# Key norms of the second block: sums with ones on the stationary side, roots and inverses on all partitions

## What is computed

```python
def rms_norm_2(x, g):
    xf = x.astype(jnp.float32)
    y = xf * lax.rsqrt(jnp.mean(xf * xf, axis=-1, keepdims=True) + EPS)
    return (y * g.astype(jnp.float32)).astype(x.dtype)

def split_kv(p_kv, k_norm_a, k_norm_b):
    b, n = p_kv.shape[:2]
    k_a, v_a, k_b, v_b = jnp.split(p_kv, [A_KV, 2 * A_KV, 2 * A_KV + B_QK], axis=-1)
    k_a = rms_norm_2(k_a.reshape(b, n, A_KV_HEADS, A_HEAD_DIM), k_norm_a)
...
    k_b = rms_norm_2(k_b.reshape(b, n, B_HEADS, 2, B_HEAD_DIM), k_norm_b)
```

## Time and profile before

| | |
|---|---|
| median of 3 runs | 2992.62 us (2988.23 to 2994.47) |
| the profiled execution | 2988.73 us |
| its span, first to last instruction | 2986.8 us |
| mean granted clock of the PE | 0.991 |
| stage `q` within it | 1463.4 to 1634.9 us |

### The profile page before, as it was taken

The page is one execution under the profiler, slowest core; times in us unless marked ns, Lnnn a source line. Parts: engine busy times, 40 slices in busy tenths (PEclk is TensorE's granted clock), DMA queues, the critical chain, the costliest instruction groups (busy, mean ns, idle before and its releaser), DMA issues.

```text
span 2986.8 us, 54566 instructions
## 1 busy us (share of the span) xinstructions
PE 2867.2 (96%) x19302; PEld 2614.9 (88%) x19302; DVE 1888.8 (63%) x2292; ACT 1595.0 (53%) x2360; POOL 787.2 (26%) x646
## 2 busy tenths in 40 slices
PE   8998899899999999999999999989989999999999
PEld 8998899898899988888888888889988888888888
DVE  5666677766677776533355666766776765555554
ACT  5555566545577765332344666665656654344443
POOL 2554234203344421121102421244424530000000
PEclk9999999999999999999999999999999999999999
DMA  7874677667777776344556655577767876666665
GB/s 264 265 241 134 204 240 240 191 183 232 242 249 244 241 240 202 95 144 146 155 167 185 191 168 161 176 241 232 243 217 243 263 257 186 188 185 188 183 187 164
DMA packets 174445, 610.65 MB, mean 204 GB/s; under 512 B 19200, under 2 KB 27520, under 8 KB 173952
## 3 DMA queue, kind: packets, MB, share of 16 engines
q1 hardware_dynamic: 161856, 589.37, 62.9%
q10 hardware_dynamic: 11152, 14.61, 1.6%
q0 software_dynamic: 1328, 5.24, 0.5%
HBM read 598.66 MB, written 5.77 MB: 202 GB/s over the span
## 4 chain that ended last, share of the span: by engine, by line
PE 70%; DVE 10%; ACT 8%; DMA 6%; issue 5%; DVEq 0%; ACTq 0%; SPq 0%
PE acc L1624 20%; PE acc L1628 19%; PE acc L1626 9%; PE acc L1627 9%; DVE wlo L1048 4%; ACT whi L603 3%; DMA raw<-w_ada 3%; ACT cond_products L599 2%; DVE conv_out L1142 1%; PE acc L1612 1%; PE acc L1614 1%; PE acc L1615 1%; PE sums L1846 1%; PE acc L1622 1%; PE sums L1682 1%
## 5 line engine op out<-in xcount | busy, mean ns | idle before, releaser
L1048 DVE TENSOR_TENSOR wlo<-raw,whi 128x1024 fp32r<-128x1024 f32 x864 | 1134.7, 1323 | 862.9 <-ACT whi L603 861.5
L603 ACT ACTIVATE whi<-raw 128x1024 fp32r<-128x1024 f32 x864 | 908.3, 1057 | 930.1 <-PE acc L1628 515.9
L1628 PE MATMUL acc<-operand,wlo 128*128 128x256 f32 (+1 forms) x4816 | 1399.0, 290 | 0.0
L1626 PE MATMUL acc<-operand,whi 128*128 128x256 f32 (+1 forms) x3136 | 938.2, 299 | 74.7 <-DVE wlo L1048 49.1
L1628 PEld LDWEIGHTS acc<-operand,wlo 128*128 128x128 f32 x4816 | 924.9, 192 | 14.3
L1627 PE MATMUL acc<-operand,whi 128*128 128x256 f32 (+1 forms) x3136 | 927.1, 296 | 0.0
L1626 PEld LDWEIGHTS acc<-operand,whi 128*128 128x128 f32 x3136 | 606.3, 193 | 99.5 <-DVE wlo L1048 48.3
L1627 PEld LDWEIGHTS acc<-operand,whi 128*128 128x128 f32 x3136 | 606.8, 194 | 12.5
L1624 PE MATMUL acc<-operand,whi 128*128 128x512 f32 x1680 | 601.6, 401 | 9.6 <-DVE operand L1392 5.9
L466 POOL TENSOR_TENSOR cond_products<-cond_products 128x512 f32<-128x512 f32 x192 | 255.6, 1331 | 1293.7 <-ACT cond_products L599 1293.1
L1624 PE MATMUL acc<-ffn_act,whi 128*128 128x512 f32 x1344 | 473.6, 396 | 3.8 <-DVE wlo L1048 3.6
(11 more groups left out here) (219 smaller groups left out, 2469.6 us busy)
## 6 DMA issues: line engine op xcount, KB each, us to landing
raw<-w_ada SPq DMA_DIRECT2D x256, 512.0 KB, 4.4
raw<-w_in SPq DMA_DIRECT2D x224, 512.0 KB, 4.0
raw<-w_up SPq DMA_DIRECT2D x176, 512.0 KB, 4.5
raw<-w_down SPq DMA_DIRECT2D x88, 512.0 KB, 4.4
raw<-w_fg SPq DMA_DIRECT2D x88, 512.0 KB, 4.2
raw<-w_fu SPq DMA_DIRECT2D x88, 512.0 KB, 3.7
raw<-w_fd SPq DMA_DIRECT2D x88, 512.0 KB, 3.5
raw<-w_o SPq DMA_DIRECT2D x32, 512.0 KB, 4.3
```

What stands on the lines that cost most here:

```text
L603: act.activation(whi[j % RING][:], raw[j % RING][:], ACT.Copy).then_inc(hi_done, 2 if st.entries[j % st.upb - 1] == (None, ADA_VEC) else 1)
L1048: dve.tensor_tensor(wlo[j % RING][:], raw[j % RING][:], whi[j % RING][:].bitcast(F32), ALU.subtract).then_inc(lo_done, 2 if prev[0] is Non ...
L1626: pe.matmul(out_, h[:, x, f], mov[:, 0], start=first, stop=False)
L1628: ins = pe.matmul(out_, l[:, x, f], mov[:, 0], start=False, stop=last)
```

## The change

The query chunks go on as before, with counters of their own order (`Q_ORDER`). For the key chunks:

- PE, steps t+3 and t+4: `key_sums`. The whole block of ones (or `halves`) is the stationary operand, two tiles of squares, 512 columns, the moving one. The result has the sum of a column on all its partitions. A chunk takes two such matmuls ("half" 0 and 1), and both write the bank `AB`, so each waits for the root of the one before (`k_root`).
- ACT, steps t+3 and t+4: the root of each half, 128x512, from `AB` to two tiles of `R` (40 to 43 for even chunks, 44 to 47 for odd ones), at the end of the step's work.
- DVE, steps t+4 (one), t+5 (two) and t+6 (one): reciprocals of the four tiles, 128x256 each, in place. At t+7 `scale_keys` reads them in place of `TP`.
- `broadcast` and its semaphore are gone. ACT's low half of the last four groups (`b >= 4`) also waits for the scaled chunks, since tiles 40 to 47 are queries' from there on. Before stage `gates` the PE waits for the values' copies and the last key root.

```diff
@@ -375,6 +376,8 @@
+        Q_ORDER = [c for c in CH_ORDER if c >= NK]
+        inverses = lambda c: 40 + 4 * (c % 2)
...
@@ -638,6 +641,8 @@
                     act.wait_ge(v2_turned, 2 * b + gb + 1)
+                    if b >= 4:
+                        act.wait_ge(n_scaled, b + 1)
...
@@ -855,19 +860,33 @@
-                    if i >= 2:
-                        act.wait_ge(n_sum, i - 1)
+                    if i >= 2 and CH_ORDER[i - 2] < NK:
+                        act.wait_ge(k_sum, 2 * CH_ORDER[i - 2] + 2)
+                    elif i >= 2:
+                        act.wait_ge(n_sum, Q_ORDER.index(CH_ORDER[i - 2]) + 1)
...
+                    if c >= NK:
+                        act.wait_ge(n_sum, Q_ORDER.index(c) + 1)
+                        act.activation(HR[:, hr_cols(c)], NB[:, hr_cols(c)], ACT.Sqrt, bias=SM[:, EPS_C:EPS_C + 1],
+                                       scale=1.0 / (64 if CH[c][1] else HD)).then_inc(n_root, 1)
+                for half in range(2):
+                    for i, c in job_at(s, 3 + half):
+                        if c < NK:
+                            act.wait_ge(k_sum, 2 * c + half + 1)
+                            act.wait_ge(v2_turned, 12 if c % 2 else 10)
+                            if c >= 2:
+                                act.wait_ge(n_scaled, c - 1)
+                            t = inverses(c) + 2 * half
+                            act.activation(R[:, t:t + 2, :], AB[:].rearrange("p (a n) -> p a n", a=2), ACT.Sqrt,
+                                           bias=SM[:, EPS_C:EPS_C + 1],
+                                           scale=1.0 / (64 if CH[c][1] else HD)).then_inc(k_root, 1)
...
@@ -1433,11 +1452,16 @@
-                dve.wait_ge(n_bcast, c + 1)
+                dve.wait_ge(k_inv, 4 * c + 4)
                 dve.scalar_tensor_tensor(
                     out=chunk, in0=chunk, scalar=gain_col("k_b" if br else "k_a", 0),
-                    in1=TP[:].rearrange("p k (a n) -> p k a n", a=2), op0=ALU.mult,
-                    op1=ALU.mult).then_inc(n_scaled, 1)
+                    in1=quad(R[:, inverses(c):inverses(c) + 4, :]), op0=ALU.mult, op1=ALU.mult).then_inc(n_scaled, 1)
+
+            def invert_keys(c, p):
+
+                root_ = R[:, inverses(c) + p, :]
+                dve.wait_ge(k_root, 2 * c + p // 2 + 1)
+                dve.reciprocal(root_, root_).then_inc(k_inv, 1)
...
+                for p, d in ((0, 4), (1, 5), (2, 5), (3, 6)):
+                    for i, c in job_at(s, d):
+                        if c < NK:
+                            invert_keys(c, p)
...
@@ -1796,32 +1823,26 @@
-            def broadcast(i, c):
...
+            def key_sums(i, c, half):
+
+                if c == half == 0:
+                    pe.wait_ge(in_rope, 48)
+                    pe.wait_ge(mods_done, st_g.ib + 1)
+                pe.wait_ge(n_sq, i + 1)
+                if c or half:
+                    pe.wait_ge(k_root, 2 * c + half)
+                pe.matmul(AB[:].rearrange("p (a n) -> p a n", a=2), halves if CH[c][1] else ones, sqb(i)[:, half, :, :],
+                          start=True, stop=True).then_inc(k_sum, 1)
 
             def norms(s):
 
+                for half in range(2):
+                    for i, c in job_at(s, 3 + half):
+                        if c < NK:
+                            key_sums(i, c, half)
                 for i, c in job_at(s, 3):
-                    head_sums(i, c)
-                for i, c in job_at(s, 7):
-                    if c < NK:
-                        broadcast(i, c)
+                    if c >= NK:
+                        head_sums(i, c)
...
@@ -1832,6 +1853,9 @@
+            pe.wait_ge(v2_copied, 12)
+            pe.wait_ge(k_root, 2 * NK)
```

More of the change, by code:

```diff
@@ L266, in build @@
         v2_turned, v2_copied = sem("v2_turned"), sem("v2_copied")
-        n_sq, n_sum, n_root, n_inv, n_scaled, n_t1, n_t2, n_rope, n_bcast, n_table, n_late = (
+        n_sq, n_sum, n_root, n_inv, n_scaled, n_t1, n_t2, n_rope, n_table, n_late = (
             sem(n) for n in ("n_sq", "n_sum", "n_root", "n_inv", "n_scaled", "n_t1", "n_t2", "n_rope",
-                             "n_bcast", "n_table", "n_late"))
+                             "n_table", "n_late"))
+        k_sum, k_root, k_inv = sem("key_sums"), sem("key_roots"), sem("key_inverse")
         k_swap = [sem(f"key_swapped{i}") for i in range(2)]
@@ L865, in norms @@
                 for i, c in job_at(s, 3):
-                    act.wait_ge(n_sum, i + 1)
                     if i == 0:
                         act.wait_ge(in_rope, 48)
-                    act.activation(HR[:, hr_cols(c)], NB[:, hr_cols(c)], ACT.Sqrt, bias=SM[:, EPS_C:EPS_C + 1],
-                                   scale=1.0 / (64 if CH[c][1] else HD)).then_inc(n_root, 1)
+                    if c >= NK:
[13 more added lines that the diff above has]
+                                           scale=1.0 / (64 if CH[c][1] else HD)).then_inc(k_root, 1)
                 for i, c in job_at(s, 9):
@@ L1450, in norms @@
                 for i, c in job_at(s, 4):
[L1451 to L1454, removed]
+                    if c >= NK:
+                        dve.wait_ge(n_root, Q_ORDER.index(c) + 1)
+                        dve.reciprocal(HR[:, hr_cols(c)], HR[:, hr_cols(c)]).then_inc(n_inv, 1)
+                        if c in TURNS_A:
+                            rotate(c)
+                for p, d in ((0, 4), (1, 5), (2, 5), (3, 6)):
+                    for i, c in job_at(s, d):
+                        if c < NK:
+                            invert_keys(c, p)
                 for i, c in job_at(s, 7):
@@ L1541, in _ @@
                     if s == AT_A - 1:
-                        dve.wait_ge(n_inv, len(JOBS))
+                        dve.wait_ge(n_inv, len(Q_ORDER))
                     attend_a(s + 1 - AT_A)
@@ L1784, in head_sums @@
             def head_sums(i, c):
-                br = CH[c][1]
+                br, n = CH[c][1], Q_ORDER.index(c)
                 pe.wait_ge(n_sq, i + 1)
[L1788 to L1791, removed]
+                if n:
+                    pe.wait_ge(n_root, n)
                 for x in range(4):
@@ L1934, in _ @@
                     if s == AT_A:
-                        pe.wait_ge(n_root, len(JOBS))
+                        pe.wait_ge(n_root, len(Q_ORDER))
                         pe.matmul(NB[:, 200:202], ones, SM[:, 28:30], start=True, stop=True).then_inc(lam_sum, 1)
```

## The result

The changed kernel takes 3002.98 us in the median of seven runs (2996.43 to 3008.71), the kernel before 2990.62 on the same chip (seven runs). The ratio is 1.0041 with a 95% interval of 1.0031 to 1.0051: 12.4 us slower, where +12.8 and a time of 3005.4 were forecast. The forecast was added to the 2992.62 of the first three runs of the kernel before; from 2990.62 it would be 3003.4. The execution that was profiled is the fastest of the seven, 2996.43 us with a span of 2994.6.

The account below looks back on a forecast made before the run. The prediction took the PE, busy 96% of the span, as the bound: -22.7 + 10.3 (PE work) + 17.6 (waits) + 7.6 (clock) = +12.8 us on 2992.6 gave 3005.4 us, range 2996 to 3013.

Parts of the forecast that it names:

- What goes, and what comes on the PE: Query projection: key column sums and spreading products go, 22.7 us; twelve 512-column matmuls come, 10.3; PE's own work falls 12.4.
- The new wait: Second halves' sums on the PE wait for ACT's first-half root through bank AB, six waits, 17.6 us in all.
- The clock: Behind the PE's idle spells in the query projection the granted clock halves: five falls of 1.5 us, 7.6 us.
- rival C: Only the two longest spells, of 3.2 us, lose the clock: +8.2 us, 3000.8 us; chance 0.10.
- ACT and DVE at nothing: In the query projection, ACT's 6.6 us more of roots and the DVE's 41.8 us of reciprocals add no further time.
- Rival E: DVE becomes the bound too, reciprocals taking half as long again beside GpSimd's rotations: 3010.4 us; chance 0.12.
- B: The PE's waits for the root come but the clock holds: +5.2 us, 2997.8 us; chance 0.13.
- D: The wait is hidden, ACT's root being done in time, leaving only the PE's saving: -12.4 us, 2980.2 us; chance 0.07.

Follow-up runs that it names:

- root first: Changed kernel with ACT taking each key half's root at the start of its step, ahead of the weight split: 2983.3 us, ratio 0.998 to the kernel before.
- two banks: Changed kernel with second halves of key sums, from chunk 1 on, in a free bank of `TP`: 2986.0 us, ratio 0.9986 to the kernel before.
- short reciprocals: Changed kernel with each of the 24 reciprocals cut to 8 of its 256 columns: 2997.27 us, ratio 1.0033 to the kernel before.
- late swap: On top of root first, the half-swapping DMAs of key chunks 2 to 5 issued two steps later: 2982.24 us, ratio 0.9983 to the kernel before.
- jobs spread: On top of root first, four jobs moved from steps 24 to 34 to 25 to 37, chunk 5 before 8: 2979.53 us, ratio 0.9971 to the kernel before.
- root behind the split: Changed kernel with ACT's key root directly behind the weight split, ahead of low half and square: 2992.39 us, ratio 1.0014 to the kernel before.
- root first and short reciprocals: Changed kernel with both edits, root at the start of ACT's step and reciprocals of 8 columns: 2977.91 us, ratio 0.9967 to the kernel before.

## Why the prediction was right, and what in it was not

**What goes, and what comes on the PE.** Right. With the waits away, two kernels give the PE's own work as 159.3 and 159.0 us against 171.5 - 12.4 = 159.1. A key sum in the changed kernel goes from 1527.35 to the next unit, whose second matmul stands at 1528.51, 0.23 behind the first: 0.93, for the 0.86 that was taken.

**The new wait.** Right in place, number and length. The spells were to read 2.8, 3.2, 2.75, 2.75, 3.2 and 1.8 and read 2.87, 3.31, 2.82, 2.82, 3.31 and 1.87: 17.0 for 16.5. The root is 0.67 for 0.68. Three edits show the mechanism: with the root first the six spells go, with a second bank for the second half the five that got it; with the root in the middle of the step they shrink by what now stands behind it. With two banks the waits went while ACT did the same work in the same order, which rules out that ACT had too little time. Its busy time in the stage rose by 5.9 us (6.6 were forecast), and cost only where it stood.

**The clock.** This is the term of the sum that was mis-sized. "I count five falls, 7.6 us" gave a fall to each of the five spells above 2.7 and none to the one of 1.8, so it went by the length of a spell. The trace of the kernel before already spoke against that: beside 2.39 with no fall stand 2.43 and 2.09 with one. The spell of 2.09 and, by windows, the clock behind it:

```profile
1195.09 8.97 PE L1682 MATMUL sums<-tiles,ident_ones 128*128 128x256 f32 x32 [2.09 <-ACT tiles L823]
...
1195.00:1200.00 5.00, 4.91 (x15) 4.01 (x16) 4.79 (x5) 2.15 (x3) 0.00 (x0) 0.66 0.00 0
```

The size of one fall was right: 1.4 to 1.6 from pairs of executions, 1.5 forecast. The number is not set by that length: the same six spells had two falls, five and two in three executions of the changed kernel and seven in the one with short reciprocals, and five spells of 1.87 had a fall each. The parts add up: 159.1 + 17.0 + 1.1 is 177.2 without falls, and with 2, 5, 2 and 7 of them at 1.5 it makes 180.2, 184.7, 180.2 and 187.7, for 180.3, 184.9, 180.2 and 187.4 measured. In the profiled execution, then, the clock took 3.0 us and not 7.6, and its stage is 180.3 long and not 184. That is rival C's size (+8.2 against +8.8 in the stage), but not its reason: the two falls stand at the spells of chunk 0 (2.87) and of the fourth (2.82), neither at one of the longest.

The stage grew by 8.8, 13.4 and 8.7 us in these three executions and the median of the whole by 12.4. The profiled execution is the fastest of seven, and in the others more falls may have come. The mean granted clock of all seven points that way: 0.988 in the two fastest (2996.43 and 2999.07 us), 0.987 in the four from 3002.48 to 3007.24, and 0.984 in the slowest, 3008.71. A thousandth of 3000 us is 3 us of full clock, or 6 us at half, about two pieces. These figures do not say where in the span the pieces lay, and in the three profiled executions the whole time did not go with the falls of the stage. So the sum of +12.8 met the median, but that it came so near was in part luck: the five falls in it were there in one profile of three. How much of the last 3.6 us is the clock in this stage and how much lies elsewhere stays open.

**ACT and DVE at nothing.** Right for this kernel, and shown for the DVE: the PE never waits for it, and 36 us off the DVE left the waits at 17.0. The reason given was right too. What covers the reciprocals is "partly the new wait itself": as soon as it was taken away, low halves of the DVE held the PE for 2.8 (root first), 3.9 (late swap) and 4.5 us (two banks) at a time. Rival E had the wrong operation in it. Reciprocals do not slow down beside GpSimd's rotations, 1.75 at the longest. The DVE's own rotations and low halves do, and E's backlog then came in the kernels in which the PE no longer waited for ACT at every key chunk.

**The rivals.** B (+5.2) falls by the ratio, whose interval begins at +9.3 us, and by the clock, which did fall; D (faster) by the ratio and the six spells. D was the side that the change could have reached: by its own condition, waits below 2.07 us a chunk with the clock held. The root-first kernel has 5.3 us of spells for six chunks and is faster though its clock fell; with the jobs spread the spells are 1.9 us and the clock held.

## What to carry to other kernels

In a program in lock step, an operation that a second engine waits for belongs at the head of the first engine's step; at the end of it, every operation ahead of it becomes the other engine's idle time, and work that engine saves (12.4 us here) can be smaller than that (17.0). Where the two halves of one job share a bank, look at what stands between them on the other engine's queue before counting what they save. And once a wait is gone, look again at the engine whose work it covered: the reciprocals that added no wait behind the others cost 6.8 us of the stage without them, and moving four job starts gave these back, as far as one profile of each tells.

## What the runs showed of the hardware that was not expected

**When the granted clock falls.** Spells of 1.87 us had the clock at half behind them five times of five (root behind the split), and the six of the changed kernel, 1.87 to 3.31 long, two, five and two pieces of 3.4 us. Before the change a spell of 2.39 had none and one of 2.09 had one. A fall is a piece of 3.4 us, at times two in a row, at 0.5, the lower of the two levels (1.2 and 2.4 GHz), and what comes ahead of it is a spell in which the PE stood. That spell can be short: with the root first and short reciprocals it was 0.67 us, then came the column sums with one moving column, and the clock fell 3 us after the spell, at 1594.0. A fall cost 1.4 to 1.6 us where two executions with the same spells could be set against each other. The length of one spell neither promises nor excludes it.

**Which VectorE work slows down beside GpSimd.** In the root-first kernel POOL rotates a key chunk from 1581.7 to 1587.5. The DVE's rotation of a query chunk beside it took 1.61 and 2.31 for its first two operations and 1.23 for the third, which ran after POOL had ended; alone each takes 1.17 to 1.23. The low half of a weight unit is of the same kind: the one that started at 1581.90 took 2.22 where 1.15 to 1.23 is usual. It is not always the DVE that is late: in the kernel with the jobs spread a low half from 1577.72 took 1.15, and POOL's operation beside it, from 1577.63, took 2.39 where others take 1.28. The 24 reciprocals of the stage stayed between 1.68 and 1.75 us, also the two from 1599.96 that ran beside POOL's next rotation (1599.34 to 1603.2):

```profile
L1468 DVE RECIPROCAL tiles<-tiles x24: 1684/1736/1749, 1509.4 to 1604.3; 128x256 f32<-128x256 f32 x24
```

The Trainium skill (SBUF — State Buffer, Who interferes with whom) says that a VectorE instruction with two SBUF inputs contends with a GpSimd instruction that reads SBUF. The trace agrees: the rotations and low halves have two inputs in SBUF and slow down (2.31 and 2.22 us), the reciprocals have one and do not (1.75 at most).
